# Second layer of a streaming encoder: keys and queries made already turned and split, kept in DRAM and loaded per head

## The reference, cut to what matters

```python
z = rmsnorm(x, kv_norm) @ w_kv_down
ckv = rmsnorm(z[..., :KV_RANK], ckv_norm)          # 256 columns
krope = rope(z[..., KV_RANK:], pos)                # 32 columns, one for all heads
kv = (ckv @ w_kv_up).reshape(bsz, t, 16, 64 + 64)  # keys and values of 16 heads
cq = rmsnorm(h @ w_q_down, q_norm)                 # 384 columns
q = (cq @ w_q_up).reshape(bsz, t, 16, 64 + 32)     # 64 plain, 32 turned by rope
logits = (q_nope . k_nope + q_rope . krope) * MLA_SCALE
p = softmax(masked logits); o = p . v
x = x + o @ w_o_b
```

## Time and profile before

| | |
|---|---|
| three runs | 1563.05, 1565.55, 1568.0 us (median 1565.55) |
| the profiled execution | 1566.23 us, span 1564.1 us |
| PE busy | 1480.1 us, 95% of the span |
| weight loads on PE | 1413.8 us, 90% |
| DVE, ACT, POOL busy | 1081.4, 729.8, 432.4 us |
| moved by DMA | 164.18 MB |

### The profile page before, as it was taken

The page is one execution under the profiler, slowest core; times in us unless marked ns, Lnnn a source line. Parts: engine busy times, 40 slices in busy tenths (PEclk is TensorE's granted clock), DMA queues, the critical chain, the costliest instruction groups (busy, mean ns, idle before and its releaser), DMA issues.

```text
span 1564.1 us, 29635 instructions
## 1 busy us (share of the span) xinstructions
PE 1480.1 (95%) x10389; PEld 1413.8 (90%) x10389; DVE 1081.4 (69%) x1962; ACT 729.8 (47%) x1510; POOL 432.4 (28%) x437
## 2 busy tenths in 40 slices
PE   8999988889899999999999997999989999999997
PEld 6788977779899999999988786999989999999997
DVE  5224267656987778787784156998598877878775
ACT  6234158754453433434252435998444343343434
POOL 0000047743422212222020004667342222222200
PEclk9999989989999999999999998999999999999998
DMA  8257566651131322313130637320022132231211
GB/s 289 99 145 210 147 186 167 165 138 48 55 109 55 106 92 68 107 54 107 56 132 19 227 121 201 94 77 1 29 81 99 64 107 82 78 107 64 97 54 61
DMA packets 129720, 164.18 MB, mean 105 GB/s; under 512 B 11936, under 2 KB 98912, under 8 KB 129648
## 3 DMA queue, kind: packets, MB, share of 16 engines
q1 hardware_dynamic: 124176, 160.62, 33.1%
q10 hardware_dynamic: 5472, 2.61, 0.9%
HBM read 132.52 MB, written 30.68 MB: 104 GB/s over the span
## 4 chain that ended last, share of the span: by engine, by line
PE 66%; issue 9%; DVE 7%; ACT 3%; DMA 3%; SPq 1%; POOL 1%; ACTq 0%; POOLq 0%; DVEq 0%
PE ps L2403 25%; PE ps L2434 21%; PE ps L1971 11%; PE ps L2137 3%; PE ps L2206 2%; PE ps L2250 1%; PE ps L2252 1%; SPq L574 1%; DMA ql<-q_turned 1%; DMA natv<-in_cache_v 1%; DVE wul L1701 1%; DVE wul L1410 1%; DVE bl L1747 1%; ACT pth L1085 1%; PE ps L2177 1%
## 5 line engine op out<-in xcount | busy, mean ns | idle before, releaser
L1799 DVE TENSOR_TENSOR xT<-xT,ps 128x592 f32<-128x592 f32 (+1 forms) x256 | 194.8, 761 | 49.0 <-PE ps L2403 47.2
L803 POOL TENSOR_TENSOR prob<-prob,rs 128x144 f32<-128x144 f32 (+4 forms) x160 | 119.4, 757 | 248.1 <-DVE rs L1562 246.5
L2434 PE MATMUL ps<-bh,wuh 128*128 128x296 f32 (+1 forms) x512 | 153.3, 299 | 8.6 <-DVE wul L1701 5.0
L2434 PE MATMUL ps<-bl,wuh 128*128 128x296 f32 (+1 forms) x512 | 152.9, 299 | 0.0
L2434 PE MATMUL ps<-bh,wul 128*128 128x296 f32 (+1 forms) x512 | 152.6, 298 | 0.0
L893 POOL TENSOR_TENSOR ssum<-raw 128x512 f32<-128x512 f32 x32 | 48.9, 1528 | 292.6 <-DMA raw<-in_w_up 290.1
L1572 DVE TENSOR_TENSOR ptl<-ps,pth 128x256 fp32r<-128x256 f32 (+2 forms) x192 | 96.1, 502 | 45.3 <-ACT pth L1085 44.6
L2403 PE MATMUL ps<-hh,dn2h 128*128 128x296 f32 (+1 forms) x512 | 111.6, 299 | 0.6 <-DVE xT L1799 0.3
L1267 ACT ACTIVATE snap<-ps 128x296 f32<-128x296 f32 (+1 forms) x32 | 13.2, 412 | 210.4 <-PE ps L2434 210.4
L2403 PE MATMUL ps<-hl,dn2h 128*128 128x296 f32 (+1 forms) x512 | 110.3, 296 | 0.0
L2403 PE MATMUL ps<-hh,dn2l 128*128 128x296 f32 (+1 forms) x512 | 110.2, 296 | 0.0
(11 more groups left out here) (284 smaller groups left out, 4589.8 us busy)
## 6 DMA issues: line engine op xcount, KB each, us to landing
raw<-in_w_up SPq DMA_DIRECT2D x32, 1024.0 KB, 7.2
raw<-in_w_down SPq DMA_DIRECT2D x32, 1024.0 KB, 5.0
raw<-in_w_in_a SPq DMA_DIRECT2D x12, 1024.0 KB, 8.5
kh<-k_turned SPq DMA_DIRECT2D x32, 212.0 KB
k_turned<-kst SPq DMA_DIRECT2D x48, 128.0 KB, 2.5
kv_mla<-stn SPq DMA_DIRECT2D x24, 256.0 KB, 2.1
q_turned<-qst SPq DMA_DIRECT2D x32, 148.0 KB, 3.1
qh<-q_turned SPq DMA_DIRECT2D x16, 296.0 KB
```

What stands on the lines that cost most here:

```text
L803: g.tensor_tensor(prob[c][0:rows, off:off + n], prob[c][0:rows, off:off + n], rs[0:rows, u:u + 1].to_broadcast([rows, n]), ALU.mult).then_ ...
L1799: v.tensor_tensor(a, a, two_banks(2 + m % 2, n), ALU.add).then_inc(x_ready if last else acc_done, 1)
L2434: i = te.matmul(ps[:, bank, 0:h], w[:, k, :], x, start=(u not in (3, 4, 6) and k == 0 and p == 0), stop=(k == 3 and p == 2), skip_group_ch ...
```

## The change

In the latent stage keys and queries are made already turned: the weights are the stationary operand, and a block holds 128 rows (two heads' 64 key or plain query numbers, or the rotary numbers of four heads) over all tokens. The columns of `w_kv_up` and `w_q_up` are put in the order that this needs when the inputs are laid out. There are now 34 blocks: four of keys (twelve matmuls each, six of 512 columns and six of 336) and seven of values (token by token as before, 512 columns), the same again for the other eight heads, and then four groups of two plain query blocks and one rotary block (18 matmuls of 296 columns each). ACT writes the high half of each key or query block and DVE the low half; for a rotary block DVE first does three multiplications with a table (`rope`), an addition, and, after ACT's copy, the subtraction. The halves go to DRAM with four DMAs a block, from two buffers for keys and three for queries; a value block goes with one DMA from one of three buffers.

The rotary keys are turned after block 22 and written to all three slots of `kh` and `kl`, which stay there. SP issues the loads of heads 0, 1 and 2 (eight DMAs each) behind the stores of block 27, and the first values behind those of block 30. The second attention takes the first one's form: three slots, one load per head, six groups of transposes a head instead of nine, no hardware loops except DVE's, values loaded by ACT with three DMAs a pair, and output weights issued behind the last head's loads. The scores keep their three passes.

```diff
+        for half in range(2):
+            LATENT += [("k", 4 * half + i) for i in range(4)] + [("v", 7 * half + t) for t in range(7)]
+        for g in range(4):
+            LATENT += [("n", 2 * g), ("n", 2 * g + 1), ("r", g)]
...
             def load_wo(layer):
-                if layer == 1:
-                    sp.wait_ge(lo_done, W_END)
                 for m in range(KD):
-                    if layer == 0 and m == 5:
-                        sp.wait_ge(s_ps, 5 * (HEADS - 1))
+                    if m == 5:
+                        sp.wait_ge(s_ps, 5 * HEADS * layer + 5 * (HEADS - 1))
...
+            def mla_head(h, c):
+                sp.dma_start(kh[c][0:HD, :].bitcast(F32), kTm[0][h]).then_inc(kq_in[c], 16)
+                sp.dma_start(qh[c][0:HD, :].bitcast(F32), qTm[0][h]).then_inc(kq_in[c], 16)
+                for x in range(2):
+                    r = HD + 16 * x
+                    sp.dma_start(qh[c][r:r + 16, :].bitcast(F32), qRm[0][x, 16 * h:16 * h + 16, :]).then_inc(kq_in[c], 16)
...
+                sp.wait_ge(kq_lo, kind_count("knr", n))
+                for low in range(2):
+                    if kind == "k":
+                        for p in range(2):
+                            sp.dma_start(kTm[low][2 * i + p], lkst[HD * p:HD * p + HD, i % 2, low, :].bitcast(F32)).then_inc(
+                                lk_out[i % 2], 16)
...
+                if n == 27:
+                    for i_ in range(2):
+                        sp.wait_ge(lk_out[i_], 64 * 4)
+                    for i_ in range(3):
+                        sp.wait_ge(lq_out[i_], LQ_COUNT[5][i_])
+                    sp.wait_ge(half_used, QU0 + 2)
+                    sp.wait_ge(kr_lo, 1)
+                    for h in range(3):
+                        mla_head(h, key_slot(h))
+                if n == 30:
+                    for i_ in range(3):
+                        sp.wait_ge(lv_out[i_], 16 * len(range(i_, 14, 3)))
+                    mla_v(sp, 0, 0, natv1[0])
+                    mla_v(sp, 1, 1, natv1[1])
...
+            for h in range(3, HEADS):
+                sp.wait_ge(s_ps, 5 * HEADS + 5 * (h - 2))
+                mla_head(h, key_slot(h))
             load_wo(1)
...
+                if kind == "k":
+                    if i >= 2:
+                        act.wait_ge(lk_out[i % 2], 64 * (i // 2))
+                    b = 2 * lat_pair(n)
+                    s.activation(lkst[:, i % 2, 0, 336:KEYS], ps[:, b, :], ACT.Copy)
+                    s.activation(lkst[:, i % 2, 0, 0:336], ps[:, b + 1, 0:336], ACT.Copy).then_inc(kq_hi, 1)
...
+                    if q >= 3:
+                        act.wait_ge(lq_out[q % 3], LQ_COUNT[q - 3][q % 3])
...
+            for i in range(3):
+                act.wait_ge(lq_out[i], LQ_COUNT[11][i])
             attention(1)
```

More of the change, by code:

```diff
@@ L458, in build, with group_at, p_split @@
         P_PARTS = [(0, 0), (1, 0), (2, 0), (3, 0), (3, 1), (NT, 0)]
[L460 to L493, removed]
+        def group_at(h, q):
+            return h * 6 + (q - 6)
+        def p_split(h, k):
+            return group_at(h, k) + 1
         okp, ovp = io["o_k_p"], io["o_v_p"]
@@ L719, in _ @@
             sp.dma_start(gq[:], io["q_norm"].partition_broadcast(P)).then_inc(rope_in, 16)
-            for j in range(QU0, W_END):
+            for j in range(QU0, QU0 + 2):
                 load(j)
@@ L739, in _ @@
[L739 to L746, removed]
-            for i in range(4):
-                sp.wait_ge(st_out[i], stored(i, N_BLK) + 16 * 12)
@@ L1100, in out, with step @@
                     s.activation(corr[rows, :], pf[0:HD, 3072:3072 + T], ACT.Copy).then_inc(o_corr, 1)
-                def fox_step(h, c, pair, first=False, last=False):
+                def step(h, c, pair, first=False, last=False):
                     if first:
-                        act.wait_ge(half_used, KVD0 - 1)
+                        act.wait_ge(half_used, W_END if layer else KVD0 - 1)
                         for u in range(3):
                             exp(h, c, u)
-                        query_hi(PAIRS - 1)
+                        if layer == 0:
+                            query_hi(PAIRS - 1)
                         exp(h, c, 3)
@@ L1350, in _, with latent_query_hi @@
[L1350 to L1354 removed]
+            def latent_query_hi(f):
+                act.wait_ge(z_out, 96)
+                act.wait_ge(zT_ps, f + 3)
+                s.activation(cqTh[:, f, :], pf[:, 2048:2048 + T], ACT.Copy).then_inc(zT_hi, 1)
@@ L1592, in fox_step @@
                         clear_prob()
-                        query_lo(PAIRS - 1)
+                        if layer == 0:
+                            query_lo(PAIRS - 1)
                         recip(h, 0)
@@ L2607, in constants, with columns @@
             e[SAM:TX, PAST + SAM:] = np.where(rm[None, :] <= rm[:, None], 0, NEG)
-    return c, m
+    rt = np.zeros((P, 2, T), np.float32)
+    at = np.concatenate([ang[t, 0:TILE_ROWS[t], :] for t in range(5)], 0).T
+    for p in range(P):
+        rt[p, 0], rt[p, 1] = np.cos(at[p % half]), np.sin(at[p % half]) * np.float32(-1 if p < HD else 1)
+    return c, m, rt
+def columns():
+    kv = [h * 2 * HD + v * HD + d for g in range(2) for v in range(2) for h in range(8 * g, 8 * g + 8) for d in range(HD)]
+    q = []
+    for g in range(4):
+        heads = range(4 * g, 4 * g + 4)
+        q += [h * R_MLA + d for h in heads for d in range(HD)]
+        q += [h * R_MLA + HD + x * (ROPE // 2) + d for x in range(2) for h in heads for d in range(ROPE // 2)]
+    return {"w_kv_up": kv, "w_q_up": q}
+COLUMNS = columns()
 _INS = [("x_prompt", "x_prompt", (SEQ, D)), ("x_sample", "x_sample", (SAM, D)), ("meta_tokens", "meta_tokens", (META, D)),
```

618 lines of the change are left out of this document (272 added, 346 removed).

## The result

The changed kernel takes 1581.41 us, median of four runs (1579.74 to 1584.57), against 1565.19 us before in the same series. The ratio is 1.0117, with a 95% interval of 1.0099 to 1.0134, so the change costs 16 us by the medians and 15 to 21 by the interval. The profiled execution took 1579.74 us (span 1577.6), 13.5 us more than that of before.

What follows compares the result with a forecast made beforehand. The second attention was taken as PE-bound. Terms 14.2 + 1.4 - 7 + 1 + 0.5 = +10.1 us on the profiled 1566.2 gave 1576.3, as median 1575.6; range 1562 to 1589, the forecast's own 1569 to 1583.

Steps and rivals of the forecast that it cites:

- The head loads ahead of the stores: Start of second attention: SP issues 24 head loads before blocks 28 to 33's stores, first exponential at 970 instead of 952.8.
- that walk: SP's issues and landings counted from block 27 to the first exponential: 970.7 us, bounds 961.5 and 980.
- The key blocks: Key and value stage: four stores a block make third and fourth key blocks late, query start 2 us later, at 908.
- a query start after 912 us: Sign that would break the step on key buffers; the query start was put at 908 us, bounds 905 and 912.
- Bytes: Rival, latent stage DMA-bound: 17.7 MB stored where 7 were, first exponential at 980 us, total 1585; chance 0.13.
- Fourth exponential to head 2: Start of second attention, up to head 2's mark: 14.8 us instead of 13.4, +1.4 (0 to +2.8).
- The pairs: Six pairs of heads in the second attention: 16.15 us a pair, 96.9 against 103.8 us, -7 (-14.4 to 0).
- the faster rival: Attention PE-bound at 14.9 us a pair and SP's issues at their short bound: total 1560; chance 0.16.
- The tail: Head 14 to the tail in second attention: +1 us (0 to +6), because the output weights arrive late.
- to the fourth: First to fourth exponential of second attention: 3.6 us instead of 6.6, without the operand transposes that lay between.
- the end: Output projection and MLP, from the tail to the kernel's end: +0.5 us.
- query blocks: Query stage: 216 matmuls of 296 columns, 29.8 us against 33.84; the 4 us gain lost behind DVE and SP.

Runs made afterwards that it cites:

- e1: Changed kernel with the loads of heads 0 to 2 issued behind the last query block's stores instead of behind block 27: 1572.3 us, ratio 1.0048.
- e4: Changed kernel with 24 more DMAs of 256 bytes issued by SP behind the 24 head loads: 1597.8 us, ratio 1.0214.
- e3: Changed kernel with key, query and rotary blocks each stored by two DMAs of 128 rows instead of four of 64: 1568.8 us, ratio 1.0019.
- e10: e3 with head 0 alone loaded behind block 27, the rest behind block 33, and the query-store wait moved from ACT to POOL: 1556.7 us.
- e9: Changed kernel with key and value blocks interleaved in each half instead of four key then seven value blocks: 1567.7 us, ratio 1.0020.
- e12: e10 plus the edits of e9 and e5, with head 0's loads ahead of block 27's stores and head 1's behind block 30's: 1541.9 us, ratio 0.9858.
- e2: Changed kernel with key blocks alone stored by two DMAs of 128 rows instead of four of 64: 1573.3 us, ratio 1.0059.
- e5: Changed kernel with the second attention's value loads of pairs 2 to 7 issued by SP instead of ACT: 1578.4 us, ratio 1.0099.
- e6: Changed kernel with five of eight output-weight pieces issued before head 4's operands instead of behind head 15's: 1582.0 us, ratio 1.0116.
- e7: e3 with a head's queries as 96 rows in DRAM, so four loads a head, and rotary blocks stored by four DMAs: 1660.4 us.

## Why the prediction was right, and where its sizes were off

- **The head loads ahead of the stores.** Right in mechanism and nearly in size: 29.7 us from PE's end to the first exponential where 28 were forecast, SP full from 941 to 973 where "938 to 965" stood. The bounds of that walk were off by 2 us: by its own terms (issues of 0.45 us and a landing of 2.3, or 0.64 and 4) they come to 963.7 and 978.1 us, not 961.5 and 980. The 974.8 measured lies within either. e1 (the order), e4 (24 issues more) and e3 (fewer issues) each moved it by what SP's issues cost. What ACT's wait for the stores before the first exponential costs by itself stays open: e10 changes it together with the order.
- **The key blocks.** The step that failed in size: "some 5 us in all" late, start of the queries 2 us later, "a query start after 912 us" as its limit. It was 8.8 us longer than before, and stood at 911.7 us only because this execution reached the stage 3 us early. The walk had the turn-round of the first half nearly right (ACT begins to empty the third and fourth key block 7.3 and 8.8 us behind the first and second in the trace, 7 predicted) but took the second half to be the same. There the same two distances are 8.1 and 10.3 us, while a piece of weights of 576 KB is loaded in between, and PE's query transposes wait 5.8 us. e9 shows that the whole loss, 12.8 us against PE's 42.1, comes from the order of the blocks. That value blocks between the key blocks would hide the stores was seen by no term of the sum.
- **Bytes.** The rival counted 17.7 MB of stores against 7, but 7 MB are the keys and values of before alone; with the queries it was 10.6. The stage was not bound by them in any case: e9 moved 259 GB/s with PE busy all the time, and e12 316 GB/s from 930 to 945 us. The share of 0.87 in the idle stretch was no bound: e1 has the first exponential 8.4 us sooner with the same bytes.
- **Fourth exponential to head 2.** +2.6 where +1.4 was forecast. The scores begin with the granted clock at its lower level, as was said (0.59 on average over the idle window, 0.50 when they begin), but that is not what the term lacked: e2, e3, e4, e5 and e9 start as low, behind 17 to 35 us without work, and take 14.4 or 14.5 us, which is +1.0 to +1.1. The other 1.6 us is the second fall of the clock at 989 us, which no term had.
- **The pairs.** 15.7 us on average and 15.57 in a steady pair, where 16.15 was forecast: a gain of 9.8 instead of 7. PE is busy 14.99 of 15.57 us, close to the 14.9 of the faster rival. The mis-sized term is the 1.25 us a pair of waits carried over from the first layer; 0.6 to 0.8 are left. e5 shows that ACT's value issues are not one of them any more.
- **The tail.** +1.9 where +1 was forecast, with the wrong reason: e6 brings the weights early and changes nothing. The extra time is the granted clock's.

Terms that were too small add up to 10.5 us (key blocks 6.7, to the first exponential 1.6, to the fourth 0.1, to head 2 1.2, tail 0.9), terms that were too large to 4.2 (pairs 2.8, the end 0.8, query blocks 0.6), and the profiled execution was 2.9 us early. With these the forecast's +10.1 becomes the 13.5 of the profiled executions; the medians are 16.2 apart. The direction and the mechanism were no luck; that the sum came out only 5.8 us under the median is luck in part, since errors of either sign cancelled.

## What to carry to other kernels

Ask of a DMA queue's engine what it asks of a compute engine: list its issues in order with their durations (0.4 to 0.6 us each here), and see who waits for the ones behind. Blocks that need a store before their buffer is free belong between blocks that don't; putting them back to back cost 12.8 us here with the same work. Count the rows of the outer dimension on both sides of a DMA before rearranging a tensor to save issues.

## What the runs showed of the hardware that was not expected

- A store of 128 rows of 3392 bytes took SP 386 ns to issue, one of 64 rows of the same length 597 ns (medians of 16 and 32). Why the longer one is cheaper was not tried.
- A DMA of 256 bytes from DRAM to DRAM took SP 589 ns (median of 24 in e4), a head's key load of 217 KB 451 ns (median of 16 in the changed kernel).
- An issue gets longer behind DMAs that are slow: of e7's first four plain stores, all of one shape, the first two took SP 0.6 and 0.5 us and the next two 2.7 and 5.8, and its first six value loads, behind such stores, 8.2 us in all where the changed kernel's took 2.9.
- The granted clock behind the same stretch of the tail (PE busy 2.2 of some 4.5 us) was 0.67 in one kernel and 1.00 in another, worth 1.6 us. Behind the fourth exponential the same happened with 0.57 and 1.00, there behind PE busy 1.96 and 2.43 of 4 us.
